# Value stage of a two-layer encoder: GpSimd takes the gate products, VectorE takes every split of a value block

## The reference, cut to what matters

```python
q = (xc @ w_q).reshape(c, PEER_HEADS, 2, PEER_HALF_DIM)
sc = jnp.einsum('chpd,hpnd->chpn', q, sub_keys)
# top 16 of each half, top 16 of their 256 sums -> experts (8 x 16 a token), out of 128 x 128
gates = jax.nn.softmax(cand_s, axis=-1)
ue = jnp.take(u, experts, axis=0)
ve = jnp.take(v, experts, axis=0)
act = jax.nn.gelu(jnp.einsum('chkd,cd->chk', ue, xc), approximate=False)
return jnp.einsum('chk,chkd->cd', gates * act, ve)
```

## Time and profile before

| | us |
|---|---|
| median of 3 runs | 3881.47 (3877.14 to 3884.13) |
| the profiled execution, its own time | 3890.68 |
| its span in the profile | 3888.9 |
| PE busy over the span | 3374.8 (87%) |
| DVE busy | 2852.5 (73%) |
| POOL busy | 1956.6 (50%) |
| ACT busy | 1401.9 (36%) |

### The profile page before, as it was taken

The page is one execution under the profiler, slowest core; times in us unless marked ns, Lnnn a source line. Parts: engine busy times, 40 slices in busy tenths (PEclk is TensorE's granted clock), DMA queues, the critical chain, the costliest instruction groups (busy, mean ns, idle before and its releaser), DMA issues. The chain is left out here.

```text
span 3888.9 us, 66686 instructions
## 1 busy us (share of the span) xinstructions
PE 3374.8 (87%) x18454; PEld 2943.5 (76%) x18454; DVE 2852.5 (73%) x5617; ACT 1401.9 (36%) x2142; POOL 1956.6 (50%) x1466
## 2 busy tenths in 40 slices
PE   8998986888969888888799989778888798888886
PEld 8877876788969766666598778777788796666664
DVE  1554177899889888888825541878998997888888
ACT  2453342434434333333224533434444343333332
POOL 3434136777613455555444331377775224555554
PEclk9999998999989999999999999889999899999998
DMA  3001236889639687788720012379895486877785
GB/s 147 20 1 60 76 122 234 298 305 313 206 92 229 232 281 279 279 280 281 248 85 12 1 60 82 115 263 307 305 312 170 119 223 238 281 280 280 280 280 192
DMA packets 402479, 765.04 MB, mean 197 GB/s; under 512 B 162400, under 2 KB 261472, under 8 KB 398432
## 3 DMA queue, kind: packets, MB, share of 16 engines
q1 hardware_dynamic: 197088, 462.06, 36.1%
q0 software_dynamic: 73728, 268.47, 18.4%
q10 hardware_dynamic: 131584, 33.56, 4.1%
HBM read 677.98 MB, written 85.98 MB: 196 GB/s over the span
## 5 line engine op out<-in xcount | busy, mean ns | idle before, releaser
L593 POOL TENSOR_TENSOR st_lo<-st_raw,st_hi 128x1024 fp32r<-128x1024 f32 x462 | 1112.8, 2409 | 986.7 <-ACT st_hi L802 983.1
L1384 PE MATMUL ps<-t_hi,st_hi 128*128 128x384 f32 (+1 forms) x2304 | 823.0, 357 | 196.2 <-POOL st_lo L593 189.3
L1386 PE MATMUL ps<-t_hi,st_lo 128*128 128x384 f32 (+1 forms) x2304 | 802.9, 348 | 0.0
L1385 PE MATMUL ps<-t_lo,st_hi 128*128 128x384 f32 (+1 forms) x2304 | 802.8, 348 | 0.0
L802 ACT CAST st_hi<-st_raw 128x1024 fp32r<-128x1024 f32 x544 | 569.5, 1047 | 222.4 <-DMA st_raw<-in_peer_u 129.6
L1384 PEld LDWEIGHTS ps<-t_hi,st_hi 128*128 128x128 f32 x2304 | 441.3, 192 | 250.2 <-POOL st_lo L593 145.3
L1646 PE MATMUL ps<-st_hi,wt_hi 128*128 128x512 f32 x1536 | 505.8, 411 | 137.7 <-DVE wt_lo L1327 127.4
L1646 PEld LDWEIGHTS ps<-st_hi,wt_hi 128*128 128x128 f32 x1536 | 269.9, 188 | 286.6 <-DVE wt_lo L1327 229.0
L1646 PE MATMUL ps<-st_lo,wt_hi 128*128 128x512 f32 x1536 | 478.1, 392 | 0.0
L1646 PE MATMUL ps<-st_hi,wt_lo 128*128 128x512 f32 x1536 | 476.1, 391 | 0.0
L1385 PEld LDWEIGHTS ps<-t_lo,st_hi 128*128 128x128 f32 x2304 | 441.4, 192 | 10.4
(11 more groups left out here) (187 smaller groups left out, 5294.1 us busy)
## 6 DMA issues: line engine op xcount, KB each, us to landing
st_raw<-in_peer_u SPq DMA_DIRECT2D x256, 512.0 KB
st_raw<-in_peer_v SPq DMA_DIRECT2D x256, 512.0 KB
gelu_d<-h_out SPq DMA_DIRECT2D x256, 192.0 KB
h_in<-gelu_d SPq DMA_DIRECT2D x256, 192.0 KB
gates_d<-g_stage ACTq DMA_DIRECT2D x32, 1024.0 KB, 9.9
g_in<-gates_d SPq DMA_DIRECT2D x256, 128.0 KB
w_raw<-in_w_in SPq DMA_DIRECT2D x16, 1168.0 KB, 5.3
st_raw<-in_peer_w_q SPq DMA_DIRECT2D x32, 512.0 KB
```

Source lines behind the costliest of these rows:

```text
L593: nc.gpsimd.tensor_tensor(st_lo[:, s].rearrange("p c f -> p (c f)"), st_raw[:, s], st_hi[:, s].rearrange("p c f -> p (c f)").bitcast(F32), ...
L1384: nc.tensor.matmul(dst, lhs[0], rhs[0], start=first, stop=False)
L1385: nc.tensor.matmul(dst, lhs[0], rhs[1], start=False, stop=False)
L1386: return nc.tensor.matmul(dst, lhs[1], rhs[0], start=False, stop=last)
```

## The change

POOL no longer splits value blocks (from block 2 on); it computes the products of gates and GELU values (`share`). DVE keeps `wt_lo`, and takes the split of every value block from block 2 on (`rest_value`). Orders change with it:

- POOL: `share(b+2)`, then `gather_v` for block b+4, for every b. `share(b)` waits for the transfers of `g_in` and `h_in` and for `wt_lo` of block b-2 (so that `w_f[s]` is free).
- DVE (`two`): for each b, `wt_lo` of block b+2, split of block b+2, `add_row(b)`.
- ACT: gated(b+2), block(b+2), for each b.
- `wt_f` and `wt_l` exchange their starting values' owners: POOL raises `wt_f` by `PRIME` at the start, DVE raises `wt_l`; PE's wait for `wt_l` is raised by the same number.

```diff
@@ POOL
-            def rest_value(i, o):
-                if o % 4 != 0:
-                    rest_block(4 * i + (QB + EB) // 2 + (o + 2) // 2, o % 2)
+            def share(b, s):
+                i = (b - s) // 2
+                pool.wait_ge(s_gh[s], (EB // 2 * l + i + 1) * 32)
+                pool.sem_inc(waited, 1)
+                pool.wait_ge(wt_l, EB * l + b + 1)
+                nc.gpsimd.tensor_tensor(w_f[:, s, 0:T_D], g_in[:, s], h_in[:, s, 0:T_D], ALU.mult)
+                nc.gpsimd.tensor_tensor(
+                    w_f[:, s, T_D:TN].rearrange("p (w o t) -> p w o t", w=2, o=1), g_stage[:, :, ds(b, 1), :],
+                    h_in[:, s, T_D:TN].rearrange("p (w o t) -> p w o t", w=2, o=1), ALU.mult).then_inc(wt_f, 1)
 
             pool.wait_ge(g_tok, TN // GRP * (l + 1) + OH_G)
             pool.sem_inc(waited, 1)
+            pool.wait_ge(g_ev, TN // GRP * (l + 1) + RING)
+            pool.sem_inc(waited, 1)
             numbers_v(0, 0)
-            for k in range(VRING):
-                gather_v(0, 0, k, first=True)
+            for b in range(VRING):
+                gather_v(0, 0, b, first=True)
+                if b < 2:
+                    share(b, b)
             with pool.Fori(0, EB // 8 - 1) as i:
                 for part in range(2):
                     g = 2 * i + 1 + part
                     numbers_v(g, 1 - part)
                     for k in range(VRING):
-                        rest_value(i, 4 * part + k)
+                        share(8 * i + 4 * part + k + 2, k % 2)
                         gather_v(g, 1 - part, k)
...
+            numbers_v(EB // 4 - 1, 1)
             for k in range(VRING):
-                rest_value(last_i, k)
-                gather_v(2 * last_i + 1, 1, k)
-            rest_value(last_i, VRING)
-            rest_value(last_i, VRING + 1)
+                share(EB - 6 + k, k % 2)
+                gather_v(EB // 4 - 1, 1, k)
+            for b in range(EB - 2, EB):
+                share(b, b % 2)
@@ ACT
-            round_gated(0, 0)
+            for b in range(2):
+                round_gated(b, b)
             with act.Fori(0, EB // 2 - 1) as i:
                 for s in range(2):
-                    round_gated(2 * i + s + 1, 1 - s)
+                    round_gated(2 * i + s + 2, s)
                     round_block(i + (QB + EB) // 2 + 1, s)
-            round_gated(EB - 1, 1)
@@ DVE
             def gated(b, s):
-                i = (b - s) // 2
-                dve.wait_ge(s_gh[s], (EB // 2 * l + i + 1) * 32)
-                dve.wait_ge(g_ev, TN // GRP * (l + 1) + RING)
-                nc.vector.tensor_tensor(w_f[:, s, 0:T_D], g_in[:, s], h_in[:, s, 0:T_D], ALU.mult)
-                nc.vector.tensor_tensor(
-                    w_f[:, s, T_D:TN]..., g_stage[:, :, ds(b, 1), :], h_in[:, s, T_D:TN]..., ALU.mult).then_inc(wt_f, 1)
                 dve.wait_ge(wt_h, EB * l + b + 1)
                 nc.vector.tensor_tensor(wt_lo[:, s], w_f[:, s], wt_hi[:, s].bitcast(F32), ALU.subtract).then_inc(wt_l, 1)
+            def rest_value(b, s):
+                dve.wait_ge(st_h, ST_PER * l + QB + EB + b + 1)
+                nc.vector.tensor_tensor(st_lo[:, s].rearrange("p c f -> p (c f)"), st_raw[:, s],
+                                        st_hi[:, s].rearrange("p c f -> p (c f)").bitcast(F32),
+                                        ALU.subtract).then_inc(st_l[s], 1)
-            def four(b, size):
-                for k in range(size):
-                    gated(b + k + 1, (k + 1) % 2)
-                    if k == 0:
-                        rest_block(QB + EB + b + 2)
-                    add_row(b + k, k)
+            def two(b, r):
+                for k in range(2):
+                    gated(b + k + 2, k)
+                    rest_value(b + k + 2, k)
+                    add_row(b + k, r + k)
@@ PE, gather
-                pe.wait_ge(wt_l, EB * l + 2 * i + s + 1)
+                pe.wait_ge(wt_l, EB * l + 2 * i + s + 1 + PRIME)
```

More of the change, by code:

```diff
@@ L441, in _ @@
         pool.sem_inc(wc_lo, PRIME)
+        pool.sem_inc(wt_f, PRIME)
         pool.sem_inc(ln_tail, 1)
@@ L674, in _ @@
                     for k in range(VRING):
-                        rest_value(i, 4 * part + k)
+                        share(8 * i + 4 * part + k + 2, k % 2)
                         gather_v(g, 1 - part, k)
-            last_i = EB // 8 - 1
-            numbers_v(2 * last_i + 1, 1)
+            numbers_v(EB // 4 - 1, 1)
             for k in range(VRING):
-                rest_value(last_i, k)
-                gather_v(2 * last_i + 1, 1, k)
-            rest_value(last_i, VRING)
-            rest_value(last_i, VRING + 1)
+                share(EB - 6 + k, k % 2)
+                gather_v(EB // 4 - 1, 1, k)
+            for b in range(EB - 2, EB):
+                share(b, b % 2)
             norm_tail(1)
@@ L929, in _ @@
         dve.sem_inc(st_l[0], 1)
-        dve.sem_inc(wt_f, PRIME)
         dve.sem_inc(v_acc, 1)
+        dve.sem_inc(wt_l, PRIME)
         dve.sem_inc(ln_done, LN_D)
@@ L1318, in gated @@
             def gated(b, s):
-                i = (b - s) // 2
-                dve.wait_ge(s_gh[s], (EB // 2 * l + i + 1) * 32)
-                dve.wait_ge(g_ev, TN // GRP * (l + 1) + RING)
-                nc.vector.tensor_tensor(w_f[:, s, 0:T_D], g_in[:, s], h_in[:, s, 0:T_D], ALU.mult)
-                nc.vector.tensor_tensor(
-                    w_f[:, s, T_D:TN].rearrange("p (w o t) -> p w o t", w=2, o=1), g_stage[:, :, ds(b, 1), :],
-                    h_in[:, s, T_D:TN].rearrange("p (w o t) -> p w o t", w=2, o=1), ALU.mult).then_inc(wt_f, 1)
                 dve.wait_ge(wt_h, EB * l + b + 1)
                 nc.vector.tensor_tensor(wt_lo[:, s], w_f[:, s], wt_hi[:, s].bitcast(F32), ALU.subtract).then_inc(wt_l, 1)
+            def rest_value(b, s):
[3 more added lines that the diff above has]
+                                        ALU.subtract).then_inc(st_l[s], 1)
             def add_row(b, r):
@@ L1335, in add_row @@
                                                op0=ALU.mult, op1=ALU.add).then_inc(v_acc, 1)
-            def four(b, size):
-                for k in range(size):
-                    gated(b + k + 1, (k + 1) % 2)
-                    if k == 0:
-                        rest_block(QB + EB + b + 2)
-                    add_row(b + k, k)
-            gated(0, 0)
-            with dve.Fori(0, EB // 4 - 1) as i:
-                four(4 * i, 4)
-            four(EB - 4, 3)
-            add_row(EB - 1, VRING - 1)
+            def two(b, r):
[3 more added lines that the diff above has]
+                    add_row(b + k, r + k)
+            for b in range(2):
+                gated(b, b)
+            with dve.Fori(0, EB // 4 - 1) as i:
+                two(4 * i, 0)
+                two(4 * i + 2, 2)
+            two(EB - 4, 0)
+            for b in range(EB - 2, EB):
+                add_row(b, b % VRING)
             for tb in range(TB + 1):
```

## The result

The changed kernel takes 4463.81 us (median of 4 runs, 4459.07 to 4467.98), against 3881.04 before: ratio 1.150, 95% interval 1.148 to 1.152, slower by 583 us. The forecast was 4424, range 4270 to 4550, 0.96 on slower. The profiled execution of the changed kernel took 4467.98 us and has a span of 4466.2 us.

A forecast was written before the change was run, and what follows sets the result against it. The prediction took a loop through POOL, ACT and DVE to bound the changed kernel at 7.1 us a block against 4.925, 271 us more a layer. With 542 us for two layers, 3881.5 became 4424 us, range 4270 to 4550.

The forecast's parts named there:

- The closed loop: Value stage: share(b+3) can't start before step b is through ACT, DVE and POOL; one turn a block; chance 0.72.
- The size of a turn, 7.1 us: Value stage: steps from share through ACT, DVE and POOL's gather sum to 7.11 us a block, against 4.925 before.
- the copy of row numbers: POOL's queue, one step in four: 0.18 us and a wait for it, taken as 0.08 us a block.
- The sum, 542 us for two layers: Whole program: each layer's value stage ends 271 us later, two layers 542 us, the rest untouched.
- 0.81 us from `add_row` to the gather, never hidden: POOL's queue: from add_row's end to the indirect transfer 0.81 us, not 0.16, because the wait is never satisfied early.
- the slow class: Rival, POOL's products: at the rate of L582, 3.213 us for 1024 columns, 1.6 instead of 1.19; 4526 us; chance 0.06.
- PE at a lower clock, at no price: PE in the value stage: gaps lower its clock to 0.6 to 0.95, without costing time.
- the ring: Value stage: the loop through POOL, ACT and DVE, taken as 7.1 us a turn, one turn for each block.
- The rival in which PE becomes the bound: Value stage: at the lower clock 18 matmuls take 7.7 us, over 7.1; if it lasted, 4573 us; chance 0.06.
- PE's own 4.40 us a block: PE in the value stage: busy share 0.894 of 4.925 us a block, so 4.40 us of work.
- the rival of a gain: Value stage: stall gone, loop doesn't close, PE binds at 4.40 us a block; 130 us off, 3751; chance 0.03.
- The exclusive lock: POOL and DVE: a GpSimd and a two-SBUF-input DVE instruction take one port pair in turns; stall 1.27 us a block.

The follow-up runs named there:

- pe_more: Six more matmuls of zeros on PE at the end of each value block, against the changed kernel: 4466.79 us, ratio to before 1.151.
- inputs_first: The changed kernel with only SP's two loads exchanged, g_in and h_in asked for before the value block: 4457.45 us, ratio to before 1.148.
- dve_fill: Against the kernel before: DVE splits every value block, its products of block b+3 stand behind wt_lo of b+2, SP's loads exchanged: 3689.87 us, ratio 0.951.
- share_ahead_in1st: The changed kernel with POOL's products one block further ahead and SP's two loads exchanged: 3733.65 us, ratio to before 0.962.
- dve_in_line: Against the kernel before: DVE splits every value block, its products right before each wt_lo, POOL only gathers: 3859.83 us, ratio 0.994.

## Why the prediction was right, point by point

- *The closed loop sets the pace.* Shown, from both sides: work added to POOL inside the loop is paid in full, work added to PE outside it is free, and shifting the products by one block takes away 536 us.
- *The size of a turn, 7.1 us.* It is 7.24. Three turns in four came as summed (1609.74 - 1602.68 = 7.06). The term that I mis-sized is the copy of row numbers: I gave it 0.08 us a block, and it is (0.19 + 0.55) / 4 = 0.19, because the product waits 0.55 us for the copy's semaphore. With the gather's 0.98 in place of 0.96 that is 0.13 of the 0.14.
- *The sum, 542 us for two layers.* In the profiled executions the last matmul of layer 2 ends 577 us later than before, 35 us more than forecast, and 248 x 0.14 = 35. The other 5 of the 40 us by which the median lies above 4424 are no part of the mechanism: I took the median 9.2 us below the profiled execution, and for the changed kernel it is 4.2. In layer 1 the last matmul ends at 2213.3 in place of 2198.2, 15 us later: 18 us by the turns, 4 us less because `share(2)` began at 1300.93 and not at 1305, and 1.4 us more behind `share(126)`. That early start is not the change's: the whole stage of layer 1 began 5 us earlier than in the trace before, its first gather at 1290.01 in place of 1295.03, and no run shows why.
- *0.81 us from `add_row` to the gather, never hidden.* Right in size, at every block. That part of it belongs to the wait and part to the indirect transfer came out only without the gathers.
- *Products at 0.73 and 0.457.* 0.748 and 0.470 in the mean; the slow class did not show. In the loop of layer 1 none was stretched, at most 0.755 and 0.483.
- *PE at a lower clock, at no price.* Right inside the ring: 0.88 in the stage, and `pe_more` shows that it costs nothing there. The rival in which PE becomes the bound did not come: PE waited for DVE's split at 113 of 122 blocks. At the end of layer 1 there is no ring left to hide it, and the last two blocks take 10.05 us where I had put 8.80. After a gap of 2.72 us the matmuls come 0.43 us apart (two in 0.85), then 0.23:

```profile
2203.26 0.98 PE L1658 MATMUL ps<-st_hi,wt_hi 128*128 128x512 f32 x2 [2.72 <-DVE st_lo L1335]
2204.04 1.05 PE L1658 MATMUL ps<-st_lo,wt_hi 128*128 128x512 f32 x2
2204.89 1.05 PE L1658 MATMUL ps<-st_hi,wt_lo 128*128 128x512 f32 x2
...
2207.23 0.63 PE L1658 MATMUL ps<-st_hi,wt_lo 128*128 128x512 f32 x2
...
2212.70 0.61 PE L1658 MATMUL ps<-st_hi,wt_lo 128*128 128x512 f32 x2
```

- *PE waits some 2.7 us a block, busy some 60%.* It waits 262.3 us at 122 blocks, 2.15 a block, and is busy 70%, 5.1 of 7.24 us. The lower clock fills the gaps, which I had named as the exception.
- *Inputs are early in the closed loop.* Right (`inputs_first`). I had not seen that they would be late as soon as the loop opens.
- *PE's own 4.40 us a block*, in the rival of a gain. Mis-sized: with no gaps a block takes 4.08. In the kernel before a block that had to wait starts slowly, and the end of its last matmul counts as busy, which between blocks without a gap lies under the next one's start. The first two matmuls take 0.58 us (1519.73 to 1520.31), the next two 0.46, and a pair's own 0.62 is 0.16 longer than its step:

```profile
1519.73 0.74 PE L1646 MATMUL ps<-st_hi,wt_hi 128*128 128x512 f32 x2 [0.88 <-DVE wt_lo L1327]
1520.31 0.62 PE L1646 MATMUL ps<-st_lo,wt_hi 128*128 128x512 f32 x2
1520.77 0.62 PE L1646 MATMUL ps<-st_hi,wt_lo 128*128 128x512 f32 x2
```

4.08 + 0.12 + 0.16 = 4.36, most of the 4.40. That rival would then have been 248 x (4.925 - 4.08) = 210 us off, 3672. `dve_fill` comes near it at 3690, by another order; with the products run ahead on POOL, as the rival had it, the best here is 3734 (`share_ahead_in1st`).

- *The exclusive lock* (the Trainium skill, SBUF — State Buffer, section "SBUF: two separate sides"). The traces agree: without POOL's splits DVE's 256-column products take 0.41 to 0.43 us in `dve_in_line`, and that kernel and its followers are faster. The gain was worth nothing behind a wait that the same change put into POOL's queue.

## What to carry to other kernels

Before work moves to an idle engine, write down what stands ahead of it in that engine's queue and what that waits for; if the moved work feeds the thing waited for, the engines take turns, and the sum of the busy times says nothing. The cure here was a place in the order, not less work: one block of distance was worth 536 us. And when a ring is opened, look for the next one, above all in the queue that starts the transfers, where a load that waits holds up one that need not.

## What the runs showed of the hardware that I had not expected

- POOL starts a product 0.40 us after the DVE instruction that it waits for, an indirect transfer 0.81 us after; in the kernel before it starts a split 0.08 us after ACT's `st_hi` (1525.19 to 1525.27). How much of this is the extra semaphore instruction in the first two stays open.
- The stall between POOL and DVE works both ways: in `share_ahead_in1st` POOL's product of 128 columns took 1.52 us beside DVE's split, where it takes 0.46 alone, and the split 1.70 in place of 1.23.
- The transfers kept up with 333 GB/s at a busy share of 0.96 in `dve_fill`, where the kernel before moved 278 at 0.79, and PE was still the bound.
